# Two shift columns and a late rms in the last feed-forward block: x times norm weight as TensorE's input

## The chip, the cores and the metric

The kernel runs on 1 core of one Trainium2 chip. The metric is the device time in microseconds (us) of one execution. Engines: TensorE (PE) multiplies matrices into PSUM, VectorE (DVE), ScalarE (ACT) and GpSimdE (POOL) work elementwise, SyncE (SP) issues the loads of the weights.

## The reference

The program is two transformer-like blocks on 256 tokens of width 1024. The change is in the last part of the second block, the convolutional feed-forward net (width 2816):

```
sh1x, sc1x, g1x, sh2x, sc2x, g2x = split(silu(c) @ w_ada + b_ada, 6)
x   = x + g1x * y_x                                   # y_x = merged @ w_o
hx2 = rms_norm(x, norm2_g) * (1 + sc2x) + sh2x        # rms_norm: x * rsqrt(mean(x*x) + 1e-6) * g
a, val = split(hx2 @ ffn_w_up)                        # 2816 columns each
a   = depthwise_conv_3x3(a as a 4 x 64 image) + conv_b
x   = x + g2x * ((gelu(a) * val) @ ffn_w_down)
return rms_norm(x, final_norm_g)
```

For one token, hx2 is r * u + s with r = rsqrt(mean(x*x) + 1e-6), u = x * norm2_g * (1 + sc2x) and s = sh2x. So hx2 @ W = r * (u @ W) + s @ W, where s @ W is the same for all tokens.

## The kernel before

**Data.** Activations lie feature by feature: a tile [128, 8, 256] holds 8 pieces of 128 features by 256 tokens. Each float32 value is split into a high half (`_hi`, rounded to float32r) and a low half (`_lo`, the rest). A product takes three matmuls: w_hi x hi, w_hi x lo, w_lo x hi (lines 359 to 361).

**Weights.** All weights come in one stream of slots, each [128, 1024]. A slot is loaded into one of 6 `raw` buffers; ScalarE writes `w_hi` (L850), VectorE or GpSimdE writes `w_lo` (L1330, L1966), each into a ring of 4. These three copies are called `fill()` in the programs of the engines. The `fill` of slot n waits on ScalarE until TensorE has used slot n - 4, and on the other engine until ScalarE is through. From the fifth slot of the last block on (`lo_by`), GpSimdE writes `w_lo` of the odd slots, so of three slots in a row it has one or two. One slot is 8 pieces x 3 = 24 matmuls.

**The last block.** Stage w_o2 makes eight tiles of x (L1448, `residual`), each with its square on ScalarE (L964) and its sum of squares on GpSimdE (L1985). Then one matmul sums over the partitions (`residual_sum`), ScalarE makes the rms factor RS (L861, L863), and VectorE and ScalarE make H2 = x * gain * RS + shift piece by piece (`norms`, L1363 and L1369; `norm_his`, L883). The 22 tiles j of the feed-forward net follow: slot "gate j", slot "up j", and, two tiles behind, slot "down j - 2". The order of TensorE is gate j, up j, down j - 2, gate j + 1, and so on. Gate j goes to PSUM bank 2p and up j to bank 2p + 1, p = j mod 2. Bank 2p is free for gate j + 2 when gelu j has read it, bank 2p + 1 for up j + 2 when G_lo of j is written. For each tile ScalarE copies the gate half into a padded image (L1294) and starts the convolution sum with the centre tap (L1295); VectorE adds the other eight taps (L1928), each waiting for the one before; ScalarE takes the gelu (L1302); VectorE multiplies by the up half (L1935); ScalarE and VectorE split the product into G_hi (L973) and G_lo (L1461), which slot "down j" multiplies into banks 4 to 7.

**Order.** Each engine has its own program with a fixed order of instructions, written out by hand; semaphores (`mark`, `past`) tie them together. Nothing is rearranged later. The two feed-forward blocks before this one (`ffn`) work in another way: their input is x times gain, without the rms, split in stage w_o while x is made (`residual_square` with `into`, `residual_low`), and RS is multiplied in behind the products.

## Time and profile before

| | us |
|---|---|
| median of 3 runs | 1184.32 |
| lowest, highest | 1183.39, 1185.36 |
| the profiled execution's own time | 1182.95 |
| its span | 1181.6 |
| TensorE busy | 1148.1 |
| VectorE busy | 832.9 |
| ScalarE busy | 618.1 |
| GpSimdE busy | 149.2 |

Times in the trace are counted from the start of the span. A matmul of 256 columns is shown with 0.28 us, but matmuls overlap: what counts is the distance from start to start. Instructions of the other engines overlap a little too when nothing lies between them. In a row of the timeline, the time in brackets is how long the engine was idle before, and what ended it.

### The profile page before, as it was taken

How to read it: one execution, taken by the hardware profiler on the slowest of the kernel's cores; microseconds unless marked ns; L12 is line 12 of the kernel's file. 1: busy time of each engine (PE TensorE's matmuls, PEld its weight loads, DVE VectorE, ACT ScalarE, POOL GpSimd, SP SyncE). 2: the span in 40 equal slices, each digit the busy share in tenths (PEclk: the TensorE clock that was granted, in tenths of full speed). 3: DMA queues.
4: the chain of work that ended last, by engine and by line, in shares of the span. 5: the costliest groups of instructions: out<-in, count | busy, mean ns of one | idle time of the engine just before them, and what ended most of it. 6: DMA issues, size and time to landing. Idle time of an engine off the chain costs nothing.

```text
span 1181.6 us, 21814 instructions
## 1 busy us (share of the span) xinstructions
PE 1148.1 (97%) x8998; PEld 1100.3 (93%) x8998; DVE 832.9 (70%) x1291; ACT 618.1 (52%) x933; POOL 149.2 (13%) x111
## 2 busy tenths in 40 slices
PE   8999899999999999999999999999999989999996
PEld 6989899999988899999999798988999978999995
DVE  5767588878675756877777775677546767767675
ACT  5655444445666655444444764755447454455553
POOL 0002101010100003110100000000000033444441
PEclk9999999999999999999999999999999989999998
DMA  8645478776534344888888545354235543555540
GB/s 314 230 143 181 157 246 286 245 256 200 168 117 147 125 167 136 286 279 278 282 267 271 209 134 171 120 166 160 92 108 176 180 161 126 181 184 176 193 142 36
DMA packets 60322, 221.36 MB, mean 187 GB/s; under 512 B 6736, under 2 KB 6992, under 8 KB 59840
## 3 DMA queue, kind: packets, MB, share of 16 engines
q1 hardware_dynamic: 59760, 218.53, 56.1%
q8 instruction: 71, 1.16, 0.4%
q10 hardware_dynamic: 288, 1.05, 0.3%
q0 software_dynamic: 176, 0.39, 0.1%
q14 instruction: 27, 0.22, 0.1%
HBM read 218.90 MB, written 1.05 MB: 186 GB/s over the span
## 4 chain that ended last, share of the span: by engine, by line
PE 89%; DVE 6%; ACT 3%; issue 1%; DMA 1%; SPq 0%; POOL 0%; ACTq 0%; DVEq 0%
PE PS L359 25%; PE PS L361 24%; PE PS L360 24%; PE PS L364 15%; ACT w_hi L850 2%; DVE w_lo L1330 1%; DVE PS L1928 1%; DMA ARENA<-memT 1%; DVE SQ L1363 1%; DVE H_lo L1373 0%; PE PS L613 0%; ACT ARENA L947 0%; DVE Y_lo L1369 0%; DVE ARENA L1956 0%; DVE ARENA L1363 0%
## 5 line engine op out<-in xcount | busy, mean ns | idle before, releaser
L1330 DVE TENSOR_TENSOR w_lo<-raw,w_hi 128x1024 fp32r<-128x1024 f32 x325 | 398.2, 1227 | 180.2 <-ACT w_hi L850 179.6
L850 ACT ACTIVATE w_hi<-raw 128x1024 fp32r<-128x1024 f32 x356 | 372.2, 1055 | 148.7 <-PE PS L361 122.7
L359 PE MATMUL PS<-Y_hi,w_hi 128*128 128x256 f32 x1240 | 356.9, 288 | 10.0 <-DVE Y_lo L1369 3.2
L360 PE MATMUL PS<-Y_lo,w_hi 128*128 128x256 f32 x1240 | 352.1, 284 | 0.0
L361 PE MATMUL PS<-Y_hi,w_lo 128*128 128x256 f32 x1240 | 352.1, 284 | 0.0
L359 PEld LDWEIGHTS PS<-Y_hi,w_hi 128*128 128x128 f32 x1240 | 238.8, 193 | 17.2 <-issue 8.1
L360 PEld LDWEIGHTS PS<-Y_lo,w_hi 128*128 128x128 f32 x1240 | 239.2, 193 | 0.4 <-issue 0.2
L361 PEld LDWEIGHTS PS<-Y_hi,w_lo 128*128 128x128 f32 x1240 | 239.0, 193 | 0.0
L359 PE MATMUL PS<-H_hi,w_hi 128*128 128x256 f32 x768 | 220.3, 287 | 4.6 <-DVE H_lo L1373 1.0
L360 PE MATMUL PS<-H_lo,w_hi 128*128 128x256 f32 x768 | 217.3, 283 | 0.0
L361 PE MATMUL PS<-H_hi,w_lo 128*128 128x256 f32 x768 | 217.2, 283 | 0.0
L359 PEld LDWEIGHTS PS<-H_hi,w_hi 128*128 128x128 f32 x768 | 147.1, 192 | 10.2 <-issue 5.2
L359 PE MATMUL PS<-G_hi,w_hi 128*128 128x256 f32 x528 | 149.6, 283 | 1.7 <-DVE w_lo L1330 1.3
L360 PE MATMUL PS<-G_lo,w_hi 128*128 128x256 f32 x528 | 149.4, 283 | 0.0
L361 PE MATMUL PS<-G_hi,w_lo 128*128 128x256 f32 x528 | 149.4, 283 | 0.0
L360 PEld LDWEIGHTS PS<-H_lo,w_hi 128*128 128x128 f32 x768 | 147.2, 192 | 0.1
L361 PEld LDWEIGHTS PS<-H_hi,w_lo 128*128 128x128 f32 x768 | 147.2, 192 | 0.0
L359 PEld LDWEIGHTS PS<-G_hi,w_hi 128*128 128x128 f32 x528 | 101.4, 192 | 2.0 <-issue 2.0
L361 PEld LDWEIGHTS PS<-G_hi,w_lo 128*128 128x128 f32 x528 | 101.4, 192 | 0.0
L360 PEld LDWEIGHTS PS<-G_lo,w_hi 128*128 128x128 f32 x528 | 101.4, 192 | 0.0
L984 ACT ACTIVATE GF<-GF 128x256 f32<-128x256 f32 x44 | 18.4, 419 | 143.5 <-DVE GF L1472 143.5
L1928 DVE SCALAR_TENSOR_TENSOR PS<-ARENA,V,PS 128x256 f32<-128x256 f32 x176 | 86.1, 489 | 5.4
(233 smaller groups left out, 1362.8 us busy)
## 6 DMA issues: line engine op xcount, KB each, us to landing
raw<-stream SPq DMA_DIRECT2D x404, 512.0 KB, 4.2
ARENA<-memT SPq DMA_DIRECT2D x2, 512.0 KB, 7.6
X<-xT SPq DMA_DIRECT2D x1, 1024.0 KB, 11.2
ARENA<-ctxT SPq DMA_DIRECT2D x1, 1024.0 KB, 5.8
ARENA<-memT SPq DMA_DIRECT2D x1, 1024.0 KB, 7.9
outT<-ARENA SPq DMA_DIRECT2D x2, 512.0 KB, 2.6
CROW<-c_rows SPq DMA_DIRECT2D x1, 512.0 KB, 10.0
ARENA<-c_rows SPq DMA_DIRECT2D x1, 512.0 KB, 12.5
```

The lines of the kernel that those rows point to most:

```text
L359: pe.matmul(o, wh, xh, start=start, stop=False, skip_group_check=True)
L360: pe.matmul(o, wh, xl, start=False, stop=False, skip_group_check=True)
L361: return pe.matmul(o, wl, xh, start=False, stop=stop, skip_group_check=True)
L364: return pe.matmul(o, w, x, start=start, stop=stop, skip_group_check=True)
L850: act.activation(w_hi[n % RING][:], raw[at][:], ACT.Copy).then_inc(*mark("hi", n))
L984: act.activation(GF[:], GF[:], ACT.Silu).then_inc(*mark("silu", l, j))
L1330: dve.tensor_tensor(w_lo[n % RING][:], raw[raw_of("slot", n)][:], w_hi[n % RING][:], ALU.subtract).then_inc(*mark("lo_dve", n))
L1363: dve.scalar_tensor_tensor(via[:, c], src[:, c], g(c), rs[1], ALU.mult, ALU.mult).then_inc(*mark("norm", tag, c))
L1928: dve.scalar_tensor_tensor(conv_sum(j), IMGS[:, j % 2, r0:r0 + ROWS, c0:c0 + COLS], gain("fconv", j + t * FC), conv_sum(j), ALU.mult, ALU. ...
```

## The change

The last block is brought to the form of the other two. U = x * norm_gain * (1 + scale) is split into U_hi and U_lo during w_o2, and is the input of gate and up, without the rms and without the shift. The shift is added as columns 256 and 257 of U (both the same), so that each product has 258 columns and column 256 is the product of the shift alone. Behind the products, VectorE multiplies each half by RS in place (`scaled`) and copies column 256 to a small tile; the gate's goes into the image as ScalarE's bias, the up's into the product with the gelu, which becomes a three-operand instruction. The centre tap is read from the image, and waits for it. U_lo of a tile of x stands on VectorE behind the next fill, that of the last one ahead of it. The sum over the squares is made inside gate 0, between pieces 5 and 6. The memset of the images goes ahead of w_o2.

In the tiles' loop the order is changed as well: on ScalarE gelu j - 1 stands ahead of image j, and G_hi of j - 1 ahead of the fills; on VectorE G_lo of j - 1 stands ahead of the taps of j.

```diff
+        U_lo, U_hi = sb("U_lo", [P, KC, T + 2], F32R), sb("U_hi", [P, KC, T + 2], F32R)
...
+        SHIFTED = small[:, 0:4]
+        SH2_COLS = MOD[:, 24:32, 0:1].to_broadcast([P, KC, 2])
+        U_TOKENS = (U_hi[:, :, 0:T], U_lo[:, :, 0:T])
...
-            residual_sum(2)
...
+            def conv_gate_up(j, ready=None, within=None):
                 p = j % 2
                 claim(2 * p)
                 assert n == gate_slot(2, j)
-                tall(PS[:, 2 * p, 0:T], H2, ready)
+                tall(PS[:, 2 * p, 0:T + 2], (U_hi, U_lo), ready, within)
                 emptied[2 * p] = [("gelu", j)]
                 claim(2 * p + 1)
-                tall(PS[:, 2 * p + 1, 0:T], H2)
+                tall(PS[:, 2 * p + 1, 0:T + 2], (U_hi, U_lo))
                 emptied[2 * p + 1] = [("g_lo", 2, j)]
 
-            conv_gate_up(0, [norm_low("norm2", k) for k in range(KC)])
+            pe.wait_ge(*past("shift_lo"))
+            conv_gate_up(0, [("h_lo", 2, k) for k in range(KC)], lambda: residual_sum(2))
...
-            project("w_o2", KC, left, then=residual_square(2))
+            act.wait_ge(*past("gs", 2))
+            act.wait_ge(*past("mod", 3))
+            act.activation(U_hi[:, :, T:T + 2], SH2_COLS, ACT.Copy).then_inc(*mark("shift_hi"))
+            project("w_o2", KC, left, then=residual_square(2, U_TOKENS, lambda c: GS[:, 2, c:c + 1]))
             inverse_rms("res2")
-            whole(norm_his("norm2", H2, lambda c: SH2(c)))
             act.preload_act_table(ACT.Gelu)
 
             def conv_gate(j):
                 b = 2 * (j % 2)
                 img = PS[:, b, 0:T].rearrange("p (r c) -> p r c", r=ROWS)
+                inner = IMGS[:, j % 2, 1:ROWS + 1, 1:COLS + 1]
+                bias = SHIFTED[:, j % 2:j % 2 + 1]
                 act.wait_ge(*past("used", gate_slot(2, j)))
+                act.wait_ge(*past("scaled", j, 0))
+                act.wait_ge(*past("bias", j, 0))
                 act.wait_ge(*past("taps", j - 2, 7) if j > 1 else past("img_zero"))
-                act.activation(IMGS[:, j % 2, 1:ROWS + 1, 1:COLS + 1], img, ACT.Copy).then_inc(*mark("img", j))
-                act.activation(conv_sum(j), img, ACT.Identity, bias=gain("fconv_b", j),
+                act.activation(inner, img, ACT.Identity, bias=bias).then_inc(*mark("img", j))
+                act.wait_ge(*past("img", j))
+                act.activation(conv_sum(j), inner, ACT.Identity, bias=gain("fconv_b", j),
                                scale=gain("fconv", j + 4 * FC)).then_inc(*mark("conv_mid", j))
...
             for j in range(FC):
+                if j:
+                    conv_value(j - 1)
                 conv_gate(j)
                 if j:
-                    conv_value(j - 1)
+                    hidden(2, j - 1)
                 fill()
                 fill()
-                if j:
-                    hidden(2, j - 1)
                 if j > 1:
                     fill()
...
-            project("w_o2", KC, residual(2, lambda c: G1(c)))
+            dve.memset(IMGS, 0.0).then_inc(*mark("img_zero"))
             dve.wait_ge(*past("gs", 2))
-            whole(norms("norm2", X, lambda c: GS[:, 2, c:c + 1], ("res2", RS[:, 0]), H2, lambda c: SH2(c)))
-            dve.memset(IMGS, 0.0).then_inc(*mark("img_zero"))
+            dve.wait_ge(*past("mod", 3))
+            dve.wait_ge(*past("shift_hi"))
+            dve.tensor_tensor(U_lo[:, :, T:T + 2], SH2_COLS, U_hi[:, :, T:T + 2],
+                              ALU.subtract).then_inc(*mark("shift_lo"))
+            project("w_o2", KC, residual(2, lambda c: G1(c)),
+                    then=residual_low(2, U_TOKENS, lambda c: GS[:, 2, c:c + 1]))
+
+            def scaled(j, i):
+                half = PS[:, 2 * (j % 2) + i, 0:T]
+                dve.wait_ge(*past("used", gate_slot(2, j) + i))
+                dve.tensor_tensor(half, half, RS[:, 0], ALU.mult).then_inc(*mark("scaled", j, i))
+                at = 2 * i + j % 2
+                dve.tensor_copy(SHIFTED[:, at:at + 1], PS[:, 2 * (j % 2) + i, T:T + 1]).then_inc(*mark("bias", j, i))
 
...
                 dve.wait_ge(*past("gelu", j))
-                dve.wait_ge(*past("used", up_slot(2, j)))
-                dve.tensor_tensor(up_product(j), PS[:, 2 * (j % 2) + 1, 0:T], GF[:],
-                                  ALU.mult).then_inc(*mark("hidden", 2, j))
-
+                dve.wait_ge(*past("bias", j, 1))
+                dve.wait_ge(*past("scaled", j, 1))
+                dve.scalar_tensor_tensor(up_product(j), PS[:, 2 * (j % 2) + 1, 0:T],
+                                         SHIFTED[:, 2 + j % 2:3 + j % 2], GF[:], ALU.add,
+                                         ALU.mult).then_inc(*mark("hidden", 2, j))
+
+            dve.wait_ge(*past("rs", "res2"))
             for j in range(FC):
+                scaled(j, 0)
                 if j:
                     conv_value(j - 1)
                 fill()
-                conv_taps(j)
-                fill()
                 if j:
                     hidden_low(2, j - 1)
+                conv_taps(j)
+                scaled(j, 1)
+                fill()
                 if j > 1:
                     fill()
```

**VectorE, the loop over the tiles.** Before, tile j = odd and then even, some way into the block. L1935 is the product of gelu and up half of the tile before, L1330 a fill, L1928 the taps, L1461 G_lo of the tile before:

```order
L1935 TENSOR_TENSOR PS<-PS,GF 128x256
L1330 TENSOR_TENSOR w_lo<-raw,w_hi 128x1024
L1928 SCALAR_TENSOR_TENSOR PS<-ARENA,V,PS 128x256 x8
L1461 TENSOR_TENSOR G_lo<-PS,G_hi 128x256
L1330 TENSOR_TENSOR w_lo<-raw,w_hi 128x1024
L1935 TENSOR_TENSOR PS<-PS,GF 128x256
L1928 SCALAR_TENSOR_TENSOR PS<-ARENA,V,PS 128x256 x8
L1330 TENSOR_TENSOR w_lo<-raw,w_hi 128x1024
L1461 TENSOR_TENSOR G_lo<-PS,G_hi 128x256
```

After, the whole odd tile 3 (to the first L1342) and the first rows of tile 4. L1941 is the product with RS, L1943 the copy of the column, L1959 the product of gelu and up half, L1473 G_lo, L1951 the taps, L1342 a fill:

```order
L1941 TENSOR_TENSOR PS<-PS,RS 128x256
L1943 COPY small<-PS 128x1
L1959 SCALAR_TENSOR_TENSOR PS<-PS,small,GF 128x256
L1473 TENSOR_TENSOR G_lo<-PS,G_hi 128x256
L1951 SCALAR_TENSOR_TENSOR PS<-ARENA,V,PS 128x256 x8
L1941 TENSOR_TENSOR PS<-PS,RS 128x256
L1943 COPY small<-PS 128x1
L1342 TENSOR_TENSOR w_lo<-raw,w_hi 128x1024
L1941 TENSOR_TENSOR PS<-PS,RS 128x256
L1943 COPY small<-PS 128x1
L1959 SCALAR_TENSOR_TENSOR PS<-PS,small,GF 128x256
L1342 TENSOR_TENSOR w_lo<-raw,w_hi 128x1024
```

A tile begins and ends its taps with a product and a copy, and G_lo and, in even tiles, a fill now stand ahead of the taps.

**ScalarE, the same loop.** Before, one tile. L1294 is the image, L1295 the centre tap, L1302 gelu of the tile before, L850 the fills, L973 G_hi of the tile before:

```order
L1294 ACTIVATE ARENA<-PS 128x4x64
L1295 ACTIVATE PS<-PS,V 128x256
L1302 ACTIVATE GF<-PS 128x256
L850 ACTIVATE w_hi<-raw 128x1024 x2
L973 ACTIVATE G_hi<-PS 128x256
L850 ACTIVATE w_hi<-raw 128x1024
```

After, one tile. L1314 is gelu of the tile before, L1305 the image, L1307 the centre tap, L978 G_hi of the tile before, L855 the fills:

```order
L1314 ACTIVATE GF<-PS 128x256
L1305 ACTIVATE ARENA<-PS,small 128x4x64
L1307 ACTIVATE PS<-ARENA,V 128x256
L978 ACTIVATE G_hi<-PS 128x256
L855 ACTIVATE w_hi<-raw 128x1024 x3
```

Gelu of the tile before moved ahead of the image, and G_hi ahead of all three fills.

**VectorE at the end of w_o2.** Before, the last two tiles of x (L1448), the fills, and the norm (L1363 by RS, L1369 with the shift):

```order
L1448 SCALAR_TENSOR_TENSOR X<-PS,MOD,X 128x256
L1330 TENSOR_TENSOR w_lo<-raw,w_hi 128x1024
L1448 SCALAR_TENSOR_TENSOR X<-PS,MOD,X 128x256
L1330 TENSOR_TENSOR w_lo<-raw,w_hi 128x1024
L1363 SCALAR_TENSOR_TENSOR SQ<-X,GS,RS 128x256 x2
L1369 SCALAR_TENSOR_TENSOR Y_lo<-SQ,MOD,Y_hi 128x256
L1363 SCALAR_TENSOR_TENSOR SQ<-X,GS,RS 128x256
```

After, the last two tiles of x (L1460) with U_lo (L1467), the fills, and the first tile of the block:

```order
L1460 SCALAR_TENSOR_TENSOR X<-PS,MOD,X 128x256
L1342 TENSOR_TENSOR w_lo<-raw,w_hi 128x1024
L1467 SCALAR_TENSOR_TENSOR U_lo<-X,GS,U_hi 128x256
L1460 SCALAR_TENSOR_TENSOR X<-PS,MOD,X 128x256
L1467 SCALAR_TENSOR_TENSOR U_lo<-X,GS,U_hi 128x256
L1342 TENSOR_TENSOR w_lo<-raw,w_hi 128x1024
L1941 TENSOR_TENSOR PS<-PS,RS 128x256
L1943 COPY small<-PS 128x1
L1342 TENSOR_TENSOR w_lo<-raw,w_hi 128x1024
```

The sixteen instructions of the norm are gone; each tile of x has its U_lo behind the next fill, and the last one has it ahead of its fill.

## Rows read from the trace of the kernel before

**Rows 1.** The page, section 1: engines' busy time, share of the span, instructions
```profile
PE 1148.1 (97%) x8998; PEld 1100.3 (93%) x8998; DVE 832.9 (70%) x1291; ACT 618.1 (52%) x933; POOL 149.2 (13%) x111
```

**Rows 2.** Windows: length, busy per engine (instructions), clock, DMA share and rate
```profile
978.00:1168.00 190.00, 186.56 (x1539) 185.98 (x1537) 136.75 (x252) 93.68 (x148) 74.55 (x31) 0.99 0.48 156
```

**Rows 3.** Timeline of TensorE: start, duration, engine, line, tiles, count [idle before <-releaser]
```profile
140.87 0.36 PE L359 MATMUL PS<-G_hi,w_hi 128*128 128x256 f32 x1 [1.30 <-DVE w_lo L1330]
...
963.83 0.28 PE L361 MATMUL PS<-H_hi,w_lo 128*128 128x256 f32 x1
...
969.45 0.55 PE L359 MATMUL PS<-Y_hi,w_hi 128*128 128x256 f32 x1 [2.75 <-DVE Y_lo L1369]
...
975.24 0.28 PE L359 MATMUL PS<-Y_hi,w_hi 128*128 128x256 f32 x1
...
989.85 0.38 PE L359 MATMUL PS<-Y_hi,w_hi 128*128 128x256 f32 x1 [2.93 <-DVE G_lo L1461]
...
990.67 0.41 PE L359 MATMUL PS<-Y_hi,w_hi 128*128 128x256 f32 x1
...
1164.85 0.28 PE L359 MATMUL PS<-G_hi,w_hi 128*128 128x256 f32 x1
```

**Rows 4.** Timeline, all engines, where the second feed-forward block starts
```profile
458.38 0.96 DVE L1455 SCALAR_TENSOR_TENSOR Y_lo<-X,V,Y_hi 128x256 fp32r<-128x256 f32 x1
...
459.26 0.41 DVE L1445 TENSOR_TENSOR X<-PS,X 128x256 f32<-128x256 f32 x1
...
460.20 0.74 POOL L1985 TENSOR_TENSOR SQ<-SQ 128x256 f32<-128x256 f32 x1 [1.15 <-ACT SQ L964]
...
464.87 0.60 PE L364 MATMUL PS<-SQ,consts 128*128 128x256 f32 x2
...
466.46 0.42 DVE L1472 TENSOR_TENSOR GF<-PS,RS 128x256 f32<-128x256 f32 x1 [3.73 <-ACT RS L863]
```

**Rows 5.** Timeline of VectorE, ScalarE and GpSimdE, a pair of tiles
```profile
1001.42 0.43 DVE L1935 TENSOR_TENSOR PS<-PS,GF 128x256 f32<-128x256 f32 x1 [1.65 <-ACT GF L1302]
...
1001.76 4.16 DVE L1928 SCALAR_TENSOR_TENSOR PS<-ARENA,V,PS 128x256 f32<-128x256 f32 x8
...
1009.19 0.53 ACT L1295 ACTIVATE PS<-PS,V 128x256 f32<-128x256 f32 x1
...
1009.64 0.39 ACT L1302 ACTIVATE GF<-PS 128x256 f32<-128x256 f32 x1
...
1009.91 1.06 ACT L850 ACTIVATE w_hi<-raw 128x1024 fp32r<-128x1024 f32 x1
...
1011.00 1.23 DVE L1330 TENSOR_TENSOR w_lo<-raw,w_hi 128x1024 fp32r<-128x1024 f32 x1 [0.51 <-ACT w_hi L850]
...
1011.85 1.06 ACT L850 ACTIVATE w_hi<-raw 128x1024 fp32r<-128x1024 f32 x1 [0.88 <-PE PS L361]
...
1012.15 4.16 DVE L1928 SCALAR_TENSOR_TENSOR PS<-ARENA,V,PS 128x256 f32<-128x256 f32 x8
...
1012.82 0.36 ACT L973 ACTIVATE G_hi<-PS 128x256 fp32r<-128x256 f32 x1
...
1012.99 2.41 POOL L1966 TENSOR_TENSOR w_lo<-raw,w_hi 128x1024 fp32r<-128x1024 f32 x1 [3.36 <-ACT w_hi L850]
...
1016.22 0.42 DVE L1461 TENSOR_TENSOR G_lo<-PS,G_hi 128x256 fp32r<-128x256 f32 x1
...
1018.70 0.43 DVE L1935 TENSOR_TENSOR PS<-PS,GF 128x256 f32<-128x256 f32 x1 [0.93 <-ACT GF L1302]
```

**Rows 6.** Timeline of GpSimdE and VectorE near 882 us
```profile
881.51 2.52 POOL L2036 TENSOR_TENSOR ARENA<-ARENA 128x512 f32<-128x512 f32 x2 [100.64 <-ACT ARENA L863]
...
883.10 2.01 DVE L1330 TENSOR_TENSOR w_lo<-raw,w_hi 128x1024 fp32r<-128x1024 f32 x1 [1.65 <-ACT w_hi L850]
```

**Rows 7.** Lines of VectorE, 30 to 36 us: shapes, busy, mean ns, idle before
```profile
L1191 ACT ACTIVATE ARENA<-PS,small 128x256 f32<-128x256 f32 x2 | 0.8, 471 | 1.5 <-DVE small L1828 1.5
...
L1828 DVE COPY small<-PS 128x2 f32<-128x2 f32 x1 | 0.1, 150 | 0.0
```

More of the change, by code:

```diff
@@ L107 @@
     "conv_act": ("img", "conv_mid"),
+    "shift_dve": ("shift_lo", "scaled", "bias"),
     "gates_act": ("vs_gelu", "u_gelu", "sig_r", "sig_a", "sig_b"),
@@ L234, in build @@
         CX = (CX_hi, CX_lo)
-        sb("above", [P, 24832 - 19584])
+        U_lo, U_hi = sb("U_lo", [P, KC, T + 2], F32R), sb("U_hi", [P, KC, T + 2], F32R)
+        sb("above", [P, 24832 - 19584 - 2 * KC * (T + 2)])
         def area(at, *shape):
@@ L813, in pe_program @@
             project("w_o2", KC, Y2, lambda i: ("added", 2, i), None, [("merged_lo", i) for i in range(KC)])
-            residual_sum(2)
-            def conv_gate_up(j, ready=None):
+            def conv_gate_up(j, ready=None, within=None):
                 p = j % 2
```

## The prediction

> **What bounds the kernel now.** I read the page first: TensorE is busy 97% of the span, 1148 of 1181.6 us [rows 1]. So only two things can move the time: less idle time of TensorE, or new idle time. Second, the timeline of TensorE around the end of w_o2 and through the last feed-forward block [rows 3]. The reader is to see a pitch of 0.12 us per matmul, 24 x 0.12 = 2.88 us per slot of weights, and two holes. The last matmul of w_o2 starts at 963.83, so gate 0, the first slot of the last block, could start at 963.95 and give way to up 0 at 966.83. But the norm lies between: gate 0 starts at 969.45, and up 0 only at 975.24. That hole costs 975.24 - 966.83 = 8.4 us, part of it because after the idle time the first matmuls run at 1.2 GHz (0.55 us where 0.28 is usual). Second hole: 2.93 us before 989.85 (the wait for G_lo of tile 0), again followed by matmuls at 1.2 GHz (0.41 us from 990.67 on, with a pitch of 0.21). Behind it none is longer than 0.4 us, and the window of the block says the same: 186.6 busy of 190 us, with VectorE at 137 and ScalarE at 94 [rows 2].
>
> Third, the other engines over one pair of tiles in that stretch [rows 5]. One pair takes 1018.70 - 1001.42 = 17.28 us = 6 slots x 2.88: TensorE sets the pace. VectorE is idle some 4 us in it. That reserve is what the change spends.
>
> **The start of the block: a gain.** Tiles U are ready slot by slot in w_o2, as they are in w_o1 before the second feed-forward block [rows 4]. There the last X (459.26) is followed by the last square sum on GpSimdE at 460.20 to 460.94, and VectorE uses the rms 1.59 us after the matmul of the sum started (466.46 - 464.87). TensorE went on without the rms. In the last block, gate 0 can start at 963.95: its bank was emptied two tiles of w_o2 earlier. The last X comes 0.3 us later than now, near 964.4, since the U_lo in front of it is held by GpSimdE, as Y_lo was, for 0.96 us, at 458.38. The square sum is then done at 964.4 + 1.68 = 966.1; TensorE reaches piece 6 at 963.95 + 18 x 0.12 = 966.1, loses at most 0.2 there and 0.4 on the sum, and ends gate 0 at 967.35. Against 975.24 this is **-7.9 us**. SH2's two columns make 258 columns of 256: in proportion 0.12 x 2/256 = 0.9 ns on 44 x 24 = 1056 matmuls, 1.0 us if TensorE still sets the pace, nothing if not. The memset (0.7 us) and the two small shift operations go to the start of w_o2, where VectorE has 0.5 us or more of idle time per slot: no cost. Squares and U_hi on ScalarE stand in idle time too, as in w_o1.
>
> **The tiles: a loss.** Added per tile on VectorE: two products with RS and two copies of one column; the value product becomes a three-operand one. Nearest rows: the product into PSUM takes 0.43 and lets the next one start after 0.34 [rows 5]. For the column copy there is one relative, two elements from PSUM in 0.15 us [rows 7]; bounds are nothing and the 0.43 of a whole product, I take 0.15, and 0.11 until the next instruction. The image on ScalarE is now Identity with a bias: between 0.39, gelu's time for as many elements out of PSUM, and the 0.53 of the centre tap with its bias [rows 5]; a ScalarE row from PSUM to SBUF with one value per partition takes 0.47 [rows 7], and I take 0.49. The centre tap now waits for it.
>
> More important is the new order of hand-overs. Before, ScalarE made the image, gelu and the first w_hi as soon as TensorE delivered, and none of them waited for VectorE's current tile. Now ScalarE's image waits for VectorE's product, and w_hi and G_hi stand behind it; VectorE's w_lo and G_lo wait for these, and the taps stand behind those. I count one tile from the start S of its first product, with hand-overs of 0.05 us:
>
> - Product 0.00, copy 0.34 to 0.49, value 0.45. ScalarE: image 0.54, centre tap 1.06, G_hi 0.45 later at 1.51 (1009.64 - 1009.19), w_hi 0.27 later at 1.78 (as behind gelu, 1009.91 - 1009.64), two more w_hi at 0.97 each (1012.82 - 1011.85).
> - Even tile (two w_lo on VectorE): w_lo waits for w_hi, 1.08 after it started (1011.00 - 1009.91): 2.86; it takes 1.15 (1012.15 - 1011.00); G_lo 4.01; taps 4.35; the eight take 4.07 (1016.22 - 1012.15): second product 8.42, copy 8.76, w_lo 8.87, end **10.02**.
> - Odd tile (one w_lo on VectorE, two on GpSimdE): G_lo waits for G_hi (1.51 + 0.36 + 0.05): 1.92; taps 2.26; second product 6.33; copy 6.67; w_lo wants to start at 6.78. GpSimdE starts its first 1.14 after ScalarE's w_hi (1012.99 - 1011.85), at 2.92, takes 2.41, and its second runs 5.33 to 7.74. A w_lo of VectorE that met GpSimdE's product took 2.01 instead of 1.23: of the overlap of 0.93 (to 884.03) it lost 0.78 [rows 6]. Here the overlap is 0.96, so I take 0.81, and the tile ends at 6.78 + 0.81 + 1.15 = **8.74**.
>
> The pair is 18.76 against TensorE's 17.28 (17.36 with 258 columns). The excess is 1.4 to 1.5 us per pair, and TensorE can't win it back: in the odd tile it waits for GpSimdE's w_lo (S + 5.4) and then for VectorE's (S + 8.8).
>
> The Trainium skill (SBUF - State Buffer, section "SBUF: two separate sides") says that a VectorE instruction with two SBUF inputs and a GpSimdE instruction take an exclusive lock for the whole instruction, and the other one blocks. By that rule the products, value, taps and G_lo, with one input in PSUM, stay free, and this w_lo is held for the whole 0.96 instead of 0.81, 0.15 us more per pair, 1.3 us over the block. The trace agrees with a block (0.78 lost of 0.93), and not with a share of the bandwidth, by which half the overlap would be lost.
>
> Start of the chain in trace time: the rms lets VectorE multiply at 966.27 + 1.59 = 967.9; ScalarE loads the gelu table until 969.15; image 0, tap, w_hi at 970.1; w_lo 971.2; taps 972.35 to 976.4. TensorE wants gate 2 at 976.0 and gets it at 977.1 (gelu 0), wants up 2 at 980.0 and gets it at 981.4, since G_lo of tile 0 stands behind w_lo at 976.85 + 4.0. Tile 1 starts at 976.85, tile 2 at 985.7 (an even tile without its last w_lo: 8.87), tile 3 at 985.7 + 10.02 = 995.7. From there nine pairs: tile 21 at 995.7 + 9 x 18.76 = 1164.5. Its G_lo is done 8.2 later (taps end 6.4, gelu, value 6.8, G_hi 7.3, G_lo 7.7 to 8.1), so the last down slot starts at **1172.7**. Before it started at 1164.85 [rows 3], and what comes behind is the same. That is +7.8 us. The last down slot also stands behind an idle time of 2.9 us (down 20 is through at S + 5.3, the last one starts at S + 8.2), as long as the one before 989.85 after which the clock fell to 1.2 GHz; a slot wholly at that clock costs 24 x 0.09 = 2.2 more, I take half: **+1.0**.
>
> Sum: -7.9 at the start, +13.3 for nine pairs (9 x 1.48), +2.4 for the start and end of the chain (the rest of the 7.8, mostly down 21, which now waits for tile 21), +1.0 for the clock: **+8.8 us**. The span goes from 1181.6 to 1190.4, the profiled time from 1182.95 to 1191.7. The median of the three runs is 1184.32, 1.4 above the profiled one; I add the difference to the median: **1193.1**.
>
> **Rivals.**
> - TensorE still sets the pace (an engine waits less than my chain says, because hand-overs overlap). It needs a pair under 17.4, 1.4 below my count. For it: VectorE's own work in a pair is only 14.9 us (my 18.76 less the waits of 2.01 for w_hi, 1.07 for G_hi and 0.81 for GpSimdE). Against: each hand-over has its row. Then the block loses as much at its start as it does now, and the change brings -7.9 + 1.0: 1184.3 - 6.9 = 1177.4. This is the case on the faster side.
> - The chain sets the pace, but GpSimdE doesn't hold VectorE in the odd tile (it comes late, or gives way). The pair is 17.95, nine are 7.3 shorter: 1193.1 - 7.3 - 1.0 (the clock, whose term rests on the idle time in front of the last slot and is as doubtful here; I leave it out) = 1184.8, no change. Rows 6 speak against it; for it only that the overlap rests on a second w_hi at the right moment.
> - The clock. Per pair TensorE idles 0.8 and 0.6 us. The 1.30 before 140.87 left it at 2.4 GHz (that matmul took 0.36), the 2.93 before 989.85 did not [rows 3]. At the start there are 1.1, 1.4 and 2.2 within 24 us. Should the clock fall for a slot each time, TensorE loses 2.2 us, of which its reserve swallows 1.4. If this happens in most pairs, or if products and copies cost 0.15 us more per tile (21 x 0.3 for two of each), the time is 1199.
>
> **Numbers.** My forecast: 60%, with a range of its own of 1188 to 1198, since 0.1 us per hand-over is 2 us over the block. TensorE sets the pace: 14%, 1177. No hold: 11%, 1185. Clock or dearer operations: 15%, 1199. About 0.2% (2.4 us) is what a measurement can tell from no change; the no-hold case alone lies in it, and partly on either side. Faster 0.16, same 0.08, slower 0.76. The range of 1183 to 1200 leaves out the TensorE case and the upper end.
>
> **What would show it.** Gate 0's first matmul within 0.2 us of the last of w_o2, and no matmul of 0.4 us or more in it. Nine pairs of 18.7 us (first product to first product, two tiles on). In every odd tile, a w_lo of VectorE of about 2.0 us that starts while GpSimdE multiplies; TensorE's waits name GpSimdE's and VectorE's w_lo, and its busy share in the block falls to some 93%. A pair of 17.3 to 17.4 would make the prediction wrong and the kernel faster by 7 us; a pair of 17.9 with w_lo of 1.23 throughout would leave the time as it was; a pair above 19.2 would put it over 1198.

## The result and the profile of the changed kernel

The changed kernel takes 1194.76 us (median of 4 runs, 1193.89 to 1196.43), the one before 1184.09 (4 runs, 1183.39 to 1185.36). The ratio is 1.0092, interval [1.0080, 1.0103]: slower, by 10.7 us. The forecast was 1193.1.

The profiled run is the slowest of the four: 1196.43, span 1194.9. Some 2.1 us of it have nothing to do with the change. In its profile the last tile of x of w_o2 starts 2.39 us later than at 964.14 before, of which 0.3 us was forecast (it stands behind a U_lo). The rest comes from code that is the same in both: 0.7 us had come about by 657 us already (a matmul that starts at 656.60 before starts at 657.25), and 1.4 us come near 682 us, where TensorE's granted clock was lower. The windows of both kernels there (length, busy time per engine with instructions, clock, DMA share and rate), first before, then after:

```profile
680.00:685.00 5.00, 5.00 (x33) 4.34 (x32) 1.61 (x2) 1.34 (x3) 0.00 (x0) 1.00 0.64 209
```

```profile
680.00:685.00 5.00, 5.00 (x25) 4.48 (x25) 2.26 (x4) 1.16 (x2) 0.00 (x0) 0.71 0.63 204
```

So the blocks are compared below by the time from the start of that last tile of x to the end of the span: 1181.6 - 964.14 = 217.5 us before, 1194.9 - 966.53 = 228.4 after, 10.9 more.

**The start of the block.** The timeline of TensorE in the changed kernel (answering [rows 3]): w_o2 ends with the row at 965.91, gate 0 starts 0.12 later, and behind the sum of the squares it goes on with its seventh piece at 968.74. The two last rows are its first waits in the block. The 0.47 of the matmul at 968.74, the one in gate 0 above the 0.4 us that the forecast allowed, is no low clock: from 969.05 on the matmuls start 0.12 apart.

```profile
965.91 0.28 PE L366 MATMUL PS<-H_hi,w_lo 128*128 128x256 f32 x1
966.03 0.28 PE L364 MATMUL PS<-U_hi,w_hi 128*128 128x258 f32 x1
...
968.42 0.67 PE L369 MATMUL PS<-SQ,consts 128*128 128x256 f32 x2
968.74 0.47 PE L364 MATMUL PS<-U_hi,w_hi 128*128 128x258 f32 x1
...
979.23 0.39 PE L364 MATMUL PS<-U_hi,w_hi 128*128 128x258 f32 x1 [0.78 <-ACT GF L1314]
...
983.70 0.39 PE L364 MATMUL PS<-U_hi,w_hi 128*128 128x258 f32 x1 [1.31 <-DVE G_lo L1473]
```

**The pairs of tiles.** The window that answers to [rows 2]: TensorE busy 176.35 instead of 186.56 of 190 us, VectorE 151.02 instead of 136.75. TensorE did less although its clock was at full speed, so it waited.

```profile
978.00:1168.00 190.00, 176.35 (x1431) 172.25 (x1431) 151.02 (x314) 90.92 (x140) 70.06 (x29) 1.00 0.45 153
```

For what, the list of TensorE's waits from 960 to 1182 says (waited for: us in total, times, longest). Before, its list for the same stretch held 3.3 us for G_lo and none for a low half of weights.

```profile
PE PS L364 <- POOL w_lo L1994: 9.4, 9, 2.1
PE PS L364 <- DVE G_lo L1473: 5.0, 3, 2.8
PE PS L364 <- DVE w_lo L1342: 2.0, 9, 0.3
PE PS L364 <- ACT GF L1314: 0.8, 1, 0.8
```

Both w_lo waits come nine times, once a pair. One of each, and the first again 18.88 us on:

```profile
1022.56 0.36 PE L364 MATMUL PS<-U_hi,w_hi 128*128 128x258 f32 x1 [0.91 <-POOL w_lo L1994]
1025.90 0.39 PE L364 MATMUL PS<-G_hi,w_hi 128*128 128x256 f32 x1 [0.22 <-DVE w_lo L1342]
1041.44 0.36 PE L364 MATMUL PS<-U_hi,w_hi 128*128 128x258 f32 x1 [0.92 <-POOL w_lo L1994]
```

The other engines from the end of an odd tile through the next even one, in the timeline (answering [rows 5]):

```profile
1041.26 2.39 POOL L1994 TENSOR_TENSOR w_lo<-raw,w_hi 128x1024 fp32r<-128x1024 f32 x1
...
1042.72 2.01 DVE L1342 TENSOR_TENSOR w_lo<-raw,w_hi 128x1024 fp32r<-128x1024 f32 x1
1044.66 0.42 DVE L1941 TENSOR_TENSOR PS<-PS,RS 128x256 f32<-128x256 f32 x1
...
1044.99 0.14 DVE L1943 COPY small<-PS 128x1 f32<-128x1 f32 x1
1045.06 0.48 DVE L1959 SCALAR_TENSOR_TENSOR PS<-PS,small,GF 128x256 f32<-128x256 f32 x1
1045.31 0.47 ACT L1305 ACTIVATE ARENA<-PS,small 128x256 f32<-128x256 f32 x1 [2.47 <-DVE small L1943]
1045.82 0.57 ACT L1307 ACTIVATE PS<-ARENA,V 128x256 f32<-128x256 f32 x1
1046.32 0.36 ACT L978 ACTIVATE G_hi<-PS 128x256 fp32r<-128x256 f32 x1
1046.59 2.94 ACT L855 ACTIVATE w_hi<-raw 128x1024 fp32r<-128x1024 f32 x3
1047.66 1.23 DVE L1342 TENSOR_TENSOR w_lo<-raw,w_hi 128x1024 fp32r<-128x1024 f32 x1 [2.13 <-ACT w_hi L855]
...
1048.80 0.42 DVE L1473 TENSOR_TENSOR G_lo<-PS,G_hi 128x256 fp32r<-128x256 f32 x1
1049.14 4.16 DVE L1951 SCALAR_TENSOR_TENSOR PS<-ARENA,V,PS 128x256 f32<-128x256 f32 x8
```

The chain is to be read downwards: VectorE's product and column copy; ScalarE's image, which had waited 2.47 us for that copy; behind it centre tap, G_hi and w_hi; and VectorE, idle for 2.13 us, waiting for w_hi with G_lo and all taps queued behind. The w_lo of 2.01 us at 1042.72 starts while GpSimdE's, of 1041.26, has 0.93 us to go.

**The end.** The last down slot starts at 1176.61 behind an idle time of 2.81 us, and 0.4 us later the matmuls take 0.41:

```profile
1176.61 0.36 PE L364 MATMUL PS<-G_hi,w_hi 128*128 128x256 f32 x1 [2.81 <-DVE G_lo L1473]
...
1177.03 0.39 PE L364 MATMUL PS<-G_hi,w_hi 128*128 128x256 f32 x1
1177.23 0.41 PE L365 MATMUL PS<-G_lo,w_hi 128*128 128x256 f32 x1
```

### The profile page after: what moved, and what is told of

The parts are those of the page before. It is cut to its first block, busy times and chain, and to the rows that moved or that the text cites. A ratio compares the mean times of both kernels' runs of the same rounds, so it can differ in the third digit from the quotient of the medians.

```text
span 1194.9 us, 21921 instructions
## 1 busy us (share of the span) xinstructions
PE 1151.5 (96%) x8998; PEld 1101.7 (92%) x8998; DVE 856.9 (72%) x1372; ACT 619.8 (52%) x934; POOL 149.5 (13%) x111
## 4 chain that ended last, share of the span: by engine, by line
PE 75%; DVE 14%; ACT 5%; issue 4%; DMA 1%; POOL 0%; ACTq 0%; SPq 0%; DVEq 0%
PE PS L364 20%; PE PS L366 20%; PE PS L365 20%; PE PS L369 15%; DVE PS L1951 7%; ACT w_hi L855 2%; DVE w_lo L1342 2%; DVE PS L1941 1%; ACT ARENA L1305 1%; DVE G_lo L1473 1%; ACT G_hi L978 1%; DMA ARENA<-memT 1%; DVE H_lo L1385 0%; PE PS L618 0%; ACT ARENA L952 0%
## 5 line engine op out<-in xcount | busy, mean ns | idle before, releaser
L1342 DVE TENSOR_TENSOR w_lo<-raw,w_hi 128x1024 fp32r<-128x1024 f32 x325 | 405.4, 1249 | 193.3 <-ACT w_hi L855 192.8
L855 ACT ACTIVATE w_hi<-raw 128x1024 fp32r<-128x1024 f32 x356 | 366.9, 1051 | 95.5 <-PE PS L366 69.5
L364 PE MATMUL PS<-Y_hi,w_hi 128*128 128x256 f32 x888 | 256.1, 288 | 5.1 <-DVE w_lo L1342 3.8
L365 PE MATMUL PS<-Y_lo,w_hi 128*128 128x256 f32 x888 | 252.6, 284 | 0.0
L366 PE MATMUL PS<-Y_hi,w_lo 128*128 128x256 f32 x888 | 252.6, 284 | 0.0
L364 PEld LDWEIGHTS PS<-Y_hi,w_hi 128*128 128x128 f32 x888 | 171.4, 193 | 11.1 <-issue 4.9
L365 PEld LDWEIGHTS PS<-Y_lo,w_hi 128*128 128x128 f32 x888 | 171.5, 193 | 0.4 <-issue 0.2
L366 PEld LDWEIGHTS PS<-Y_hi,w_lo 128*128 128x128 f32 x888 | 171.5, 193 | 0.0
L364 PE MATMUL PS<-U_hi,w_hi 128*128 128x258 f32 x352 | 100.8, 286 | 11.6 <-POOL w_lo L1994 9.4
L366 PE MATMUL PS<-U_hi,w_lo 128*128 128x258 f32 x352 | 99.2, 282 | 0.0
```

What stands on the lines that cost most here:

```text
L364: pe.matmul(o, wh, xh, start=start, stop=False, skip_group_check=True)
L365: pe.matmul(o, wh, xl, start=False, stop=False, skip_group_check=True)
L366: return pe.matmul(o, wl, xh, start=False, stop=stop, skip_group_check=True)
L855: act.activation(w_hi[n % RING][:], raw[at][:], ACT.Copy).then_inc(*mark("hi", n))
L1342: dve.tensor_tensor(w_lo[n % RING][:], raw[raw_of("slot", n)][:], w_hi[n % RING][:], ALU.subtract).then_inc(*mark("lo_dve", n))
```

## The experiments

Ten kernels ran. Times are medians; "block" is, as above, the time from the last tile of x of w_o2 to the end of the span in the profile. Six of the ten differ in nothing but three edits: the norm behind the products (with the early start that it makes possible), the loops' new order, and all low halves of the block on GpSimdE. With the two kernels of the case these are all eight combinations:

| norm behind the products | new order | all w_lo on GpSimdE | time, us | ratio to before, 95% | block, us |
|---|---|---|---|---|---|
| no | no | no (before) | 1184.1 | | 217.5 |
| no | yes | no | 1178.03 | 0.9952 [0.9940, 0.9964] | 212.1 |
| no | no | yes | 1180.03 | 0.9964 [0.9952, 0.9976] | 212.4 |
| no | yes | yes | 1178.70 | 0.9947 [0.9935, 0.9959] | 211.2 |
| yes | no | no | 1207.05 | 1.0195 [1.0168, 1.0222] | 241.1 |
| yes | yes | no (the change) | 1194.76 | 1.0092 [1.0080, 1.0103] | 228.4 |
| yes | no | yes | 1176.93 | 0.9943 [0.9927, 0.9960] | 208.6 |
| yes | yes | yes | 1171.21 | 0.9890 [0.9871, 0.9909] | 203.8 |

The blocks are each read from one profile and hold a difference that no edit made: the sums behind the last down slot ran at 1.2 GHz in some profiles and at 2.4 in others. From the last down slot to the end of the span are 15.8 to 15.9 us in six of the twelve profiles, and 16.5 to 16.9 in the others, not counting 1.5 us in two of them (the change and the run with GpSimdE's short w_lo), whose last down slot itself ran mostly at 1.2 GHz. So a block is good to about 1 us only, and where it matters the time to the start of the last down slot is given instead.

### All low halves on GpSimdE, in the changed kernel

```diff
-    return "lo_pool" if n % 2 and n >= AT["ffn2"] + RING else "lo_dve"
+    return "lo_pool" if n >= AT["ffn2"] + RING else "lo_dve"
```

> The changed kernel, but GpSimdE writes the low half of every slot of the last block from the fifth on (64 of 66 slots less the first), VectorE none. Theory (VectorE's chain through w_hi, w_lo and taps sets the pace): a tile on VectorE shrinks to about 6.9 us (G_lo at S + 2.1, taps 2.4 to 6.5, product and copy 0.4), GpSimdE needs 3 x 2.4 = 7.2 us per tile, TensorE 8.66, so TensorE sets the pace again, no VectorE w_lo is left that could be held, and the waits of gate 2 and up 2 go too. The last down slot then starts 64 slots x 2.9 after gate 0: about 1172 us (1170 to 1177), faster than both kernels. Rival (the hand-over from VectorE's product through ScalarE sets the pace, whoever writes the low half, or GpSimdE is too slow at this): stays above 1186.

Measured: 1171.21 us (1168.9 to 1172.3), ratio 0.989. In its list of waits TensorE waits for nothing between 960 and the last sums, and two value products of VectorE stand 8.61 us apart (1006.11 and 1014.72). The mechanism is the one expected: VectorE is out of TensorE's path, and the start of the block keeps its gain (up 0 starts 3.73 us behind the last matmul of w_o2, 3.74 in the change, 11.41 before). This version beats both kernels of the case.

### GpSimdE's colliding w_lo made short

The second low half that GpSimdE makes in an odd tile j, that of gate j + 2, covers 128 of 1024 columns (the rest of it is left out of the result). This holds from gate 5 on, so for the nine odd tiles 3 to 19.

```diff
                     pool.wait_ge(*past("hi", n))
-                    pool.tensor_tensor(w_lo[n % RING][:], raw[raw_of("slot", n)][:], w_hi[n % RING][:],
-                                       ALU.subtract).then_inc(*mark("lo_pool", n))
+                    at = n - AT["ffn2"]
+                    cols = 128 if at % 6 == 1 and at >= 13 else D
+                    pool.tensor_tensor(w_lo[n % RING][:, 0:cols], raw[raw_of("slot", n)][:, 0:cols],
+                                       w_hi[n % RING][:, 0:cols], ALU.subtract).then_inc(*mark("lo_pool", n))
```

> The changed kernel, but from tile 5 on GpSimdE's second low half in each odd tile (the next but one gate slot, 9 slots in all) is written for 128 of its 1024 columns only; the rest of that low half is left as it was. It ends before VectorE's own w_lo wants to start, and nothing else changes. Theory (GpSimdE holds VectorE for 0.8 us in each odd tile): all of VectorE's w_lo take 1.23, the pair falls from 18.88 to 18.1, the time by 9 x 0.8 = 7 us to about 1187.5. Rival (the hold is beside the path that sets the end): 1194 to 1195.

Measured: 1188.23 (1187.14 to 1189.69), ratio 1.0037 [1.0024, 1.0050]. Its timeline of VectorE in the odd tile and the start of the two even ones around it:

```profile
1041.45 0.48 DVE L1959 SCALAR_TENSOR_TENSOR PS<-PS,small,GF 128x256 f32<-128x256 f32 x1
...
1058.00 1.21 DVE L1342 TENSOR_TENSOR w_lo<-raw,w_hi 128x1024 fp32r<-128x1024 f32 x1
1059.53 0.48 DVE L1959 SCALAR_TENSOR_TENSOR PS<-PS,small,GF 128x256 f32<-128x256 f32 x1
```

The w_lo takes 1.21 instead of 2.01, and the pair 1059.53 - 1041.45 = 18.08 instead of 18.88: what the w_lo gains, the pair gains whole. The nine pairs come to 7.1 us in the profile, from the last matmul of w_o2 to the last down slot (203.56 instead of 210.70). The medians differ by 6.5, and the runs of either kernel spread over 2.5 us. The hold is real and sits in the chain; without it the change is still slower than the kernel before.

### VectorE's first w_lo behind the taps

```diff
                 if j:
                     conv_value(j - 1)
-                fill()
-                if j:
                     hidden_low(2, j - 1)
                 conv_taps(j)
                 scaled(j, 1)
+                fill()
                 fill()
```

> The changed kernel, but VectorE's first fill of a tile stands behind the taps and not ahead of G_lo and taps; VectorE does the same work. Theory (in even tiles VectorE waits 2.1 us for w_hi with the taps behind it): G_lo in even tiles as early as in odd ones, the pair falls by 0.94 to 17.9, the time by 8.5 to 10 us to about 1185. TensorE's wait then names VectorE's w_lo ahead of up slots. Rival (TensorE needs that w_lo early, so that the wait only changes its place): 1192 or more.

Measured: 1190.87 (1189.33 to 1191.98), ratio 1.0056 [1.0041, 1.0071]: 3.9 us less than the change, not 8.5 to 10. That expectation failed. The wait for w_hi went, as intended, but the pair is 18.83 us. The timeline of GpSimdE and VectorE in an odd tile says why:

```profile
1040.00 2.39 POOL L1993 TENSOR_TENSOR w_lo<-raw,w_hi 128x1024 fp32r<-128x1024 f32 x1 [0.86 <-ACT w_hi L855]
1040.55 2.93 DVE L1342 TENSOR_TENSOR w_lo<-raw,w_hi 128x1024 fp32r<-128x1024 f32 x1
```

VectorE's w_lo now starts 1.84 us before GpSimdE's ends (not 0.93), and takes 2.93 instead of 1.21: the hold has grown from 0.80 to 1.72, and with 1.19 us of waiting for G_hi in both tiles (1.18 in one before) this eats what the wait of 2.13 gave back. TensorE now waits for VectorE's w_lo, 1.37 us a pair; the next run shows that it is late only because it is held. What is left lies at the two ends: the last down slot starts 3.2 us earlier behind w_o2 than in the change, nearly all of it won before the pairs, and it runs at 2.4 GHz, behind an idle time of 0.63 instead of 2.81 us.

### The same with GpSimdE's w_lo short

To test that reading, both edits above together (the short low half leaves out what it left out there).

> The changed kernel with the first w_lo of VectorE behind the taps (as in the run of 1190.87 us) and, from tile 5 on, only 128 of 1024 columns in GpSimdE's second w_lo of the odd tiles (the rest of that low half is left out). In the run of 1190.87 us the wait for w_hi was gone, but the pair stayed at 18.83, since the w_lo of the odd tile took 2.90 to 2.93 instead of 1.22. Theory (it is held for the 1.8 us in which GpSimdE's product is still under way): with the short product that w_lo takes 1.2 to 1.5, the pair falls to TensorE's 17.4, eight pairs give 11 us, time 1180. Rival (the pair is set by something else, as the waits of 1.19 for G_hi in both tiles): pair over 18.3, 1187 or more.

Measured: 1176.61 (1175.98 to 1177.91), ratio 0.9940 [0.9925, 0.9955]; against 1190.87 that is 14.3 us less, where 11 were expected. The value products at 1048.30 and 1065.51, a pair apart, are 17.21 apart: TensorE sets the pace, and its busy time from 1000 to 1150 is 150.00 of 150. The waits of 1.19 for G_hi are still there, so they weren't the cause; the held w_lo was. All products, copies and low halves of VectorE are still done here, so its work alone is not what made the pair 18.88. The first row below is two w_lo back to back, both unheld:

```profile
1045.63 2.35 DVE L1342 TENSOR_TENSOR w_lo<-raw,w_hi 128x1024 fp32r<-128x1024 f32 x2
1048.30 0.48 DVE L1959 SCALAR_TENSOR_TENSOR PS<-PS,small,GF 128x256 f32<-128x256 f32 x1
...
1054.78 1.22 DVE L1342 TENSOR_TENSOR w_lo<-raw,w_hi 128x1024 fp32r<-128x1024 f32 x1
```

### The old order, with the norm behind the products

The loops of ScalarE and VectorE in the old order: image, centre tap, gelu, w_hi, G_hi on ScalarE, and G_lo behind the taps on VectorE (the core of the edit on ScalarE):

```diff
             for j in range(FC):
+                conv_gate(j)
                 if j:
                     conv_value(j - 1)
-                conv_gate(j)
+                fill()
+                fill()
                 if j:
                     hidden(2, j - 1)
-                fill()
-                fill()
```

> The changed kernel without its second part: on ScalarE the image and centre tap stand ahead of gelu j - 1 again and G_hi behind two fills, on VectorE G_lo stands behind the taps and the fills. Theory (the loss comes from the products by RS and the image's wait for them, the reorder softens it): gelu is now 1.0 us later in each tile and the value product with the taps behind it waits for it, the pair grows by 0.4 to 19.3 us, the time to about 1198. Rival (the reorder is what costs, since it puts G_lo and w_lo ahead of the taps): near 1184.

Measured: 1207.05 (1203.47 to 1211.25), ratio 1.0195 [1.0168, 1.0222]: 12.3 us over the change, where some 3 were expected. The direction was right and the size was not. VectorE's timeline over one tile and into the next:

```profile
1063.76 3.43 DVE L1342 TENSOR_TENSOR w_lo<-raw,w_hi 128x1024 fp32r<-128x1024 f32 x1
1067.12 0.41 DVE L1473 TENSOR_TENSOR G_lo<-PS,G_hi 128x256 fp32r<-128x256 f32 x1
1067.45 0.41 DVE L1941 TENSOR_TENSOR PS<-PS,RS 128x256 f32<-128x256 f32 x1
1067.78 0.14 DVE L1943 COPY small<-PS 128x1 f32<-128x1 f32 x1
1069.51 0.49 DVE L1959 SCALAR_TENSOR_TENSOR PS<-PS,small,GF 128x256 f32<-128x256 f32 x1 [1.58 <-ACT GF L1314]
1070.46 1.22 DVE L1342 TENSOR_TENSOR w_lo<-raw,w_hi 128x1024 fp32r<-128x1024 f32 x1 [0.46 <-ACT w_hi L855]
```

The value product waits 1.58 us in every tile for a gelu that stands behind the image, and the w_lo of one tile in two meets a GpSimdE product, in most pairs for longer than in the changed kernel: 3.43 here, 2.74 to 2.79 in others. From the value product at 1008.23 to the one at 1161.26 are 15 tiles of 10.20, so a pair is 20.4, 1.5 over the changed kernel. Nine of these are 13.7 us. TensorE waits 2.2 to 2.7 us at a time, and from 980 to 995 its clock is 0.66 to 0.83 in windows of 5 us. I had counted a later gelu, and neither the longer overlap with GpSimdE nor the clock.

In four tiles of this run the two engines start within 0.03 us of each other. In two of them VectorE is held (the w_lo of 3.43), in the other two GpSimdE, 3.48 us instead of 2.40, while VectorE's w_lo keeps its time:

```profile
1004.47 3.48 POOL L1994 TENSOR_TENSOR w_lo<-raw,w_hi 128x1024 fp32r<-128x1024 f32 x1 [1.44 <-ACT w_hi L855]
```

```profile
1004.49 1.22 DVE L1342 TENSOR_TENSOR w_lo<-raw,w_hi 128x1024 fp32r<-128x1024 f32 x1
```

### The new order alone, in the kernel before

The edit of the loops' order, made in the kernel before; the norm stays where it was.

> The kernel before with nothing but the new order of the loops: gelu, G_hi and G_lo of the tile behind stand ahead of the taps. Theory (before, TensorE sets the pace of the pairs, so the order can only shorten the idle time of 2.93 us before 989.85, where G_lo of tile 0 stands behind the taps of tile 1, and the 1.2 GHz behind it): 3 us less, 1181, pair still 17.28. Rival (the order is worth nothing where VectorE has a reserve): 1184. Rival (gelu ahead of the image makes ScalarE late, as in the changed kernel): slower than 1186.

Measured: 1178.03 (1177.3 to 1181.09), ratio 0.9952 [0.9940, 0.9964], 5.7 us by the ratio, where 3 were expected. TensorE does not wait for G_lo of tile 0 any more, and from 978 to 1000 it is busy all the time at full clock (first the window of the kernel before, 19.07 us busy at 0.92, then that of this one):

```profile
978.00:1000.00 22.00, 19.07 (x147) 18.86 (x146) 17.38 (x32) 9.08 (x14) 7.20 (x3) 0.92 0.41 128
```

```profile
978.00:1000.00 22.00, 22.00 (x185) 21.92 (x184) 15.86 (x30) 10.05 (x17) 7.41 (x3) 1.00 0.40 123
```

The last square sums start at 1167.26, which is 1167.26 - 966.19 = 201.07 behind the last tile of x; before, 1169.67 - 964.14 = 205.53. So 4.5 us are gone there: the idle 2.93, another wait of 0.39 for G_lo at 1161.90, and 1.5 for the matmuls 0.21 apart behind the hole, less a new wait of 0.24 for w_lo at 1009.69. I had counted the hole and not the clock. A further 0.9 of the block's difference lies in the tail, where the sum with RS takes 0.70 us at 2.4 GHz and took 1.22 before; that varies from profile to profile in untouched code, and it is not shown that the order has a part in it. The pairs are 17.28 as before (1050.43 to 1067.71).

### All low halves on GpSimdE, in the kernel before

> The kernel before with every low half of the last block's weights on GpSimdE. Theory (this pays only where VectorE is in the chain that TensorE waits for; before, it is not): within 1.5 us of before, 1183.5, pair still 17.28. Rival (the 1171.2 of the changed kernel with all low halves on GpSimdE came from the move itself and has nothing to do with the norm behind the products): 1172.

Measured: 1180.03 (1179.78 to 1180.54), ratio 0.9964 [0.9952, 0.9976], 4.3 us faster where under 1.5 was expected. The pair is 17.28, as expected (1042.02 to 1059.30). The gain comes from the same hole: G_lo of tile 0 has no w_lo in front of it any more, and TensorE waits for it at 988.74 for 0.30 us instead of 2.93. So it's not the pace of the pairs, but my expectation of under 1.5 was wrong: I had looked at the pairs and forgotten the hole. In the profile the last down slot starts 4.1 us earlier behind w_o2.

### New order and all low halves on GpSimdE, in the kernel before

> The kernel before with the new order and with all low halves on GpSimdE: everything of the 1171.2 us version except the norm behind the products. Theory (the start of the block is worth 7.9 us and needs the norm behind the products): 1180, so 8 to 9 us over that version. Rival (the late norm adds nothing to the other two edits): 1172.

Measured: 1178.70 (1175.72 to 1179.82), ratio 0.9947 [0.9935, 0.9959]. The two edits take away the same hole and don't add up. Against the version of 1171.21 the block is 211.2 - 203.8 = 7.4 us longer, and the median 7.5. This is what the early start of the block is worth when nothing else is late. It can be read directly: up 0 starts 11.40 us behind the last matmul of w_o2 here and 3.73 there, so 7.7 us are won before up 0. From up 0 to the last down slot are 184.31 and 183.84 us. The tail, at 2.4 GHz here and at 1.2 there, hides 1.0 of the gain in these two profiles.

### The change without its products

The products with the rms, the column copies and the two biases are left out, and with them the norm's rms and shift; the early start and the order stay.

One of the edited places:

```diff
             def scaled(j, i):
-                half = PS[:, 2 * (j % 2) + i, 0:T]
-                dve.wait_ge(*past("used", gate_slot(2, j) + i))
-                dve.tensor_tensor(half, half, RS[:, 0], ALU.mult).then_inc(*mark("scaled", j, i))
-                at = 2 * i + j % 2
-                dve.tensor_copy(SHIFTED[:, at:at + 1], PS[:, 2 * (j % 2) + i, T:T + 1]).then_inc(*mark("bias", j, i))
+                pass
...
```

> The changed kernel without the products by the rms, the column copies and the biases of the last block (the norm's scale and shift are left out of the result; the early start and the order stay). Theory (the added work of VectorE per tile and its place ahead of ScalarE's image make the pair 18.88 us long): the pair falls to TensorE's 17.3 to 17.4, the start keeps its 7.9 us, time 1173. Rival (the longer pair comes from the low halves' collision and the new order alone): pair over 18, 1184 or more.

Measured: 1173.46 (1171.14 to 1174.76), ratio 0.9906 [0.9893, 0.9919]. The pair is 17.21 (value products at 1042.66 and 1059.87), and TensorE is busy 149.77 of the 150 us from 1000 on, against 139.61 in the change. So 21 us hang on four products and four columns a pair, directly or through what they shift. Their own time, from the start of a product to the start of what follows its copy, is 4 x 0.40 = 1.6 us a pair, and VectorE stands idle for 4.05 us a pair here (3.29 for w_hi, 0.56 for G_hi, 0.20 for gelu), so it could carry them. One part of the rest is the hold, which is gone here as well: VectorE's w_lo takes 1.22 in both tiles, since GpSimdE's product no longer meets it (0.80 of the 1.67 us that the pair loses). The other part I put down to where the products stand, ahead of ScalarE's image and all that is queued behind it. No run moved them alone; what supports it is the run of 1176.61, where all of them are done and the pair is 17.21 once VectorE is not held and doesn't wait for w_hi.

### All low halves on GpSimdE, with the old order

> The version with all low halves on GpSimdE (1171.2 us), with the old order of the loops. With the old order the value product waits 1.58 us per tile for a gelu that stands behind image and centre tap. Theory (without low halves VectorE needs 6.9 us of a tile's 8.64, so 1.6 us of waiting just fit): TensorE still sets the pace in the pairs, but the idle time for G_lo of tile 0 is back: 1175, at most 1180. Rival (the order is worth 12 us, as between the changed kernel and its undone order, 1207): 1183 or more.

Measured: 1176.93 (1176.52 to 1177.85), ratio 0.9943 [0.9927, 0.9960]. The value products still wait 1.59 us each (1038.73, 1047.34, 1055.94), but they come every 8.60 us: the waits fit into VectorE's reserve. What remains of the order is at the two ends, in TensorE's timeline:

```profile
979.39 0.39 PE L364 MATMUL PS<-U_hi,w_hi 128*128 128x258 f32 x1 [0.61 <-ACT GF L1314]
...
984.71 0.39 PE L364 MATMUL PS<-U_hi,w_hi 128*128 128x258 f32 x1 [2.14 <-DVE G_lo L1473]
...
1156.04 0.36 PE L364 MATMUL PS<-G_hi,w_hi 128*128 128x256 f32 x1 [1.82 <-DVE G_lo L1473]
```

That is 4.6 us for gelu 0, G_lo of tile 0 and the G_lo of tile 20; the clock stays at 1.00 behind all three. The order is worth 12.3 us in the changed kernel, where VectorE sets the pace, 5.7 here and about as much in the kernel before, where TensorE does, and no more than 1.3 in the kernel before with all low halves on GpSimdE (1180.03 to 1178.70), which had already lost the hole.

## Why the prediction came out right

Its sum was +8.8; the runs say +10.7. Step by step:

- **Start of the block, -7.9 forecast.** Gate 0 starts with no gap (966.03 behind 965.91). Its 24 matmuls give way to up 0 at 969.65 (six from 968.74 on: 968.74, 969.05, then 0.12 apart), less the 2.08 of delay from elsewhere 967.57, forecast 967.35. So -7.7, and the same 7.7 up to up 0 between the two versions that differ in it alone.
- **Pair of tiles, 18.76 forecast.** Measured 18.88: even 10.07 (10.02 forecast), odd 8.80 (8.74). The image starts 0.65 after the product, not 0.54, and the centre tap takes 0.57 with its source in SBUF, not 0.53. The column copy takes 0.15 and the image 0.476, near the estimates (0.15 and 0.49). Nine pairs make 1.1 us of the miss.
- **The hold, 0.81 forecast.** 0.80 by the experiment that removed it. The rule of the Trainium skill (SBUF - State Buffer, "SBUF: two separate sides"), an exclusive lock for the whole instruction, would have made it 0.93 for the overlap of 0.93. Over four overlaps of these runs the held time, over the 1.21 of a free one, is 0.80 of 0.93, 1.53 of 1.66 (old order, w_lo of 2.74), 1.72 of 1.84 and 2.22 of 2.35 (VectorE from 1063.76, GpSimdE until 1066.11): always 0.12 to 0.13 less than the overlap. So the rule holds, less a constant; a share of the bandwidth it is not.
- **258 columns, 1.0 forecast if TensorE sets the pace.** Not seen as a loss: where it does, a pair takes 17.21 with U and its 258 columns, and 17.28 before. Within one kernel the wider ones do take a little longer: in the run of 1171.21 a matmul comes 0.1197 us after the one before in gate and up (258 columns) and 0.1192 in down (256). Before, it is 0.1200 in all; why that is more is open.
- **Start and end of the chain, +2.4 forecast.** Gates and ups were late in the order forecast: gate 2 at 979.23 for gelu 0 (977.1 + 2.08 = 979.18 forecast), up 2 at 983.70 for G_lo (981.4 + 2.08 = 983.48). Tile 3 started at 998.11 - 2.08 = 996.03 instead of 995.7, and the last down slot at 1176.61 - 2.08 = 1174.5 instead of 1172.7: 1.1 from the pairs, 0.3 and 0.4 from the two ends.
- **The clock, +1.0 forecast.** From the last down slot to the end of the span are 18.29 us, before 16.75: +1.5, where half a slot was taken. Of its 24 matmuls 16 took 0.39 to 0.41; the first three and the last five were at full speed.

Together, less the delay of 2.08, these make 11.2 us in the profile, 2.4 over the sum: all four terms, start, pairs, ends and clock, came out dearer than forecast, by 0.2 to 1.1 us each.

The rivals: that TensorE keeps the pace fell with the waits list; it came true only where VectorE lost its low halves or its products, or where neither the hold nor the wait for w_hi was left. That there is no hold fell with a w_lo of 1.99 to 2.03 us in each odd tile from 3 to 19. Low clocks after each wait fell too: waits of 0.9 and 2.1 us left the clock at 1.00, and only the one of 2.81 was followed by 1.2 GHz.

What the prediction did not draw from its own [rows 3]: the hole of 2.93 us before 989.85, which it names, was in the kernel before to be had for an order of instructions, without any late norm, and with its clock it is worth 4.5 us in the profile (the kernel became 5.7 us faster). In the sum it is contained (the block of the changed kernel is counted from its own chain), but told as one change, the two halves pulled in opposite directions: the order alone 5.7 us faster, the norm behind the products 16.7 us slower on top of it (1194.76 - 1178.03). Taken the other way round, the norm alone costs 23 us (1207.05), and the order then gives 12.3 back.

## What to carry to other kernels

Scaling after the product instead of before frees the start of a stage, but puts two more steps of the busiest helper engine ahead of everything that another engine does for each tile; count the whole round of hand-overs per tile, not that engine's busy time (VectorE was busy 151 of 190 us here, and TensorE waited all the same). Where such a round is longer than TensorE's tile, give the helper's independent work (here the low halves) to the idle engine first: the same late norm, in the new order, is then worth 7.5 us instead of costing 16.7. And a wait removed by reordering can come back as a longer collision of two engines on SBUF; look at what the moved instruction now meets.

## What the runs showed of the hardware

- An instruction of VectorE with both inputs in SBUF that starts while GpSimdE works on SBUF is held for the overlap less 0.12 to 0.13 us (four overlaps of 0.93 to 2.35 us). GpSimdE can be the one held, too: four times in these runs a w_lo of VectorE that started within 0.1 us of GpSimdE's product kept its 1.22, and the product took 3.39 to 3.48 instead of 2.40. The taps, products and G_lo, with one input in PSUM, kept their time (0.489, 0.425 and 0.42 us) beside GpSimdE's product.
- Matmuls with 258 columns cost next to nothing over those with 256: 0.1197 us from start to start against 0.1192 in one kernel. A pair of tiles in which 96 of the 144 matmuls have 258 takes 17.21 us, against 17.28 (0.1200) in the kernel with 256 in all. I have no explanation for the 0.07 less.
- A column of one element per partition copied from PSUM takes 0.15 us, and the next instruction starts 0.07 after its start.
- ScalarE's activation with a scale and a bias per partition, SBUF to PSUM, takes 0.570 us; the same one from PSUM took 0.53 [rows 5].
- In 8 of the 12 profiles TensorE's granted clock between 680 and 690 us is 0.66 to 0.83, in the other 4 it is 1.00, in code that no edit touched. In the changed kernel's profile this stretch costs 1.4 us. How much of the spread between runs of one kernel comes from it is not shown, since one run of each was profiled.
- The length of TensorE's idle time alone does not say whether the clock falls. In the changed kernel with the old order the same wait of 2.20 us was followed by a clock of 1.00 (from 1026.3 and 1067.5 on) and by 0.54 (from 1046.3 and 1087.6 on).
